# Conditioning vectors 6, 7 and 16 summed by TensorE in six halves instead of by VectorE in 24 blocks

## The reference

```python
cond = jax.nn.silu(c)
for l in range(DEPTH):
    m = (cond @ w_mod[l] + b_mod[l]).reshape(bsz, 3, 3, D_MODEL)
    x = x + 0.5 * m[:, 0, 2][:, None] * swiglu(adaln_in(x, norm_g[l, 0], m, 0), ...)
    h = adaln_in(x, norm_g[l, 1], m, 1) @ w_in[l]
    ...
    x = x + m[:, 1, 2][:, None] * (mix @ w_out[l])
    x = x + 0.5 * m[:, 2, 2][:, None] * swiglu(adaln_in(x, norm_g[l, 2], m, 2), ...)
```

## Time and profile before

| | us |
|---|---|
| median of 3 executions | 1642.44 (1641.61 to 1642.79) |
| the profiled execution, its own time | 1640.37 |
| its span in the trace | 1638.6 |
| TensorE matmuls busy | 1460.2 (89% of the span) |
| TensorE weight loads busy | 1375.4 (84%) |
| VectorE busy | 1361.1 (83%) |
| ScalarE busy | 982.0 (60%) |
| GpSimd busy | 81.9 (5%) |
| DMA | 420.31 MB, mean 257 GB/s over the span |

### The profile page before, as it was taken

The page is one execution under the profiler, slowest core; times in us unless marked ns, Lnnn a source line. Parts: engine busy times, 40 slices in busy tenths (PEclk is TensorE's granted clock), DMA queues, the critical chain, the costliest instruction groups (busy, mean ns, idle before and its releaser), DMA issues.

```text
span 1638.6 us, 27675 instructions
## 1 busy us (share of the span) xinstructions
PE 1460.2 (89%) x11160; PEld 1375.4 (84%) x11160; DVE 1361.1 (83%) x2231; ACT 982.0 (60%) x1640; POOL 81.9 (5%) x153
## 2 busy tenths in 40 slices
PE   7989758798979888887999999999999999988997
PEld 4888657697969786766998998987999899868997
DVE  2999758899999999877888988686988888687886
ACT  4555536555566446545676766547766766577665
POOL 0113010001101110000000000000000000000000
PEclk9999979899999999998999999899999999799999
DMA  9999563679968994427886877334777677435773
GB/s 387 366 385 415 204 235 140 251 289 333 392 237 323 402 395 155 154 77 284 284 317 227 281 276 262 123 148 170 267 273 272 231 276 278 162 116 199 274 273 129
DMA packets 84972, 420.31 MB, mean 257 GB/s; under 512 B 9363, under 2 KB 9795, under 8 KB 58094
## 3 DMA queue, kind: packets, MB, share of 16 engines
q1 hardware_dynamic: 64478, 343.48, 57.7%
q0 software_dynamic: 20368, 75.06, 12.1%
HBM read 417.38 MB, written 1.13 MB: 255 GB/s over the span
## 4 chain that ended last, share of the span: by engine, by line
PE 41%; DVE 6%; ACT 3%; DMA 2%; issue 1%; DVEq 0%
PE pw L626 13%; PE pw L627 13%; PE acc L626 6%; PE acc L627 6%; DVE low_p L1953 2%; DMA land_d<-stream 1%; ACT h_hi L1358 1%; PE acc L905 1%; PE pw L863 1%; ACT hi_p L1456 1%; ACT sq L1361 0%; PE acc L885 0%; DMA land_p<-stream 0%; ACT hi_d L1456 0%; DVE low_d L1953 0%
## 5 line engine op out<-in xcount | busy, mean ns | idle before, releaser
L626 PE MATMUL pw<-h_hi,hi_p 128*128 128x256 f32 x2976 | 754.3, 292 | 49.8 <-DVE low_p L1953 27.1
L627 PE MATMUL pw<-h_lo,low_p 128*128 128x256 f32 x2976 | 742.9, 288 | 0.0
L626 PEld LDWEIGHTS pw<-h_hi,hi_p 128*128 128x128 f32 x2976 | 587.1, 197 | 69.3 <-issue 30.1
L627 PEld LDWEIGHTS pw<-h_lo,low_p 128*128 128x128 f32 x2976 | 587.3, 197 | 0.4 <-issue 0.2
L1953 DVE SCALAR_TENSOR_TENSOR low_p<-hi_p,land_p 128x1024 fp32r<-128x1024 f32 x418 | 506.8, 1221 | 42.4 <-ACT hi_p L1456 42.1
L1456 ACT ACTIVATE hi_p<-land_p 128x1024 fp32r<-128x1024 f32 x418 | 434.0, 1047 | 64.4 <-DMA land_p<-stream 64.3
L626 PE MATMUL acc<-a_hi,hi_d 128*128 128x256 f32 x1376 | 343.2, 287 | 47.0 <-DVE low_d L1953 35.5
L627 PE MATMUL acc<-a_lo,low_d 128*128 128x256 f32 x1376 | 339.4, 284 | 0.0
L626 PEld LDWEIGHTS acc<-a_hi,hi_d 128*128 128x128 f32 x1376 | 265.4, 193 | 54.9 <-issue 41.1
L627 PEld LDWEIGHTS acc<-a_lo,low_d 128*128 128x128 f32 x1376 | 265.7, 193 | 0.0
L1953 DVE SCALAR_TENSOR_TENSOR low_d<-hi_d,land_d 128x1024 fp32r<-128x1024 f32 x205 | 249.4, 1218 | 11.7 <-ACT hi_d L1456 11.6
(11 more groups left out here) (354 smaller groups left out, 1665.7 us busy)
## 6 DMA issues: line engine op xcount, KB each, us to landing
land_p<-stream SPq DMA_DIRECT2D x207, 1024.0 KB, 5.1
land_d<-stream SPq DMA_DIRECT2D x209, 512.0 KB, 5.6
modw<-wmod POOLq DMA_DIRECT2D x116, 512.0 KB, 8.5
biasT<-wmod POOLq DMA_DIRECT2D x12, 512.0 KB, 4.2
biasT<-bias_rows POOLq DMA_DIRECT2D x3, 1536.0 KB, 11.4
modw<-wmod SPq DMA_DIRECT2D x8, 512.0 KB, 7.6
biasT<-wmod SPq DMA_DIRECT2D x8, 512.0 KB, 10.7
biasT<-bias_rows POOLq DMA_DIRECT2D x1, 3072.0 KB, 13.5
```

The source lines that it names most:

```text
L626: mm(o, lhs[0], rhs[0], start=start, stop=False, skip_group_check=True)
L627: return mm(o, lhs[1], rhs[1], start=False, stop=stop, skip_group_check=True)
```

## The change

Vectors 6, 7 and 16 leave VectorE's list (24 of its 128 blocks). Each is made by TensorE in two halves of 512 outputs: (6, 0), (6, 1), (7, 0), (7, 1), (16, 0), (16, 1). A half is four transfers of 512 KB, `half_sums` (eight calls, like those of `mod_first`), `half_copy` on ScalarE (128 x 512), `half_turn` on TensorE (four calls with one column) and `half_total` on VectorE (128 x 4). `STREAMED` puts (6, 0) and (6, 1) into steps 9 and 18 of stage 0 and (16, 0) and (16, 1) into steps 8 and 15 of stage 3: sums ahead of `up(j)`, copy behind `a_hi` of step j, turn behind `up(j + 1)`, total behind the gating product of step j + 1. (7, 0) takes the place of `keep_busy`; (7, 1) stands behind chunk 4. Their eight loads are issued ahead of the bias rows. The loads of the other four halves stand one by one between the loads for VectorE. In stage 0 VectorE now has 32 blocks, all eight of vector 6 being loaded there too; in stage 3 it has 32 instead of 40; in the mixer none.

The diff, cut:

```diff
-MOD_AT = {0: [[]] + spread(2, 7, 20, 4) + [[]], 2: [[]] * 3 + spread(8, 12, 17) + [[]] * 2,
-          3: [[]] * 3 + spread(12, 17, 17) + [[]] * 2, 5: [[]] * 3 + spread(17, 18, 18) + [[]]}
+MOD_AT = {0: [[]] + spread(2, 6, 20) + [[]], 2: [[]] * 3 + spread(8, 12, 17) + [[]] * 2,
+          3: [[]] * 3 + spread(12, 16, 17) + [[]] * 2, 5: [[]] * 3 + spread(17, 18, 18) + [[]]}
 RAW = (2, 3, 5)
-MOD_FIRST = {min(some[0] for some in MOD_AT[i] if some): i for i in (2, 5)}
-_ab = iter([(6, k) for k in range(4, KD)] + [(7, k) for k in range(KD)])
-MOD_AB = {(back, b): [next(_ab) for _ in range(count)] for back, b, count in AB_MODS}
+SUMMED = [2, 3, 4, 5] + list(range(8, 16)) + [17]
+HALVES = ((6, 0), (6, 1), (7, 0), (7, 1), (16, 0), (16, 1))
+HALF_NO = {half: x for x, half in enumerate(HALVES)}
+STREAMED = {0: {9: (6, 0), 18: (6, 1)}, 3: {8: (16, 0), 15: (16, 1)}}
+MOD_FIRST = {(8, 0): 2, (17, 0): 5}
...
+        def half_slot(x, n):
+
+            if HALVES[x] == (7, 0):
+                return modw[:, n, :]
+            if HALVES[x] == (7, 1) and n < 2:
+                return (proj[:, 18:22, :], qb[:])[n].rearrange("p c s -> p (c s)")
+            return wide_slot(n)
...
+            def load_half(g, h, n):
+
+                x = HALF_NO[g, h]
+                if (g, h) == (7, 0):
+                    pool.wait_ge(mod_used, 4 * KD - MODR + n + 1)
+                elif x:
+                    pool.wait_ge(mod_taken, 2 * KD + 4 * (x if (g, h) != (7, 1) else 2))
+                pool.dma_start(half_slot(x, n), wmod[g, 4 * h + n]).then_inc(half_load[x], 16)
...
-            load_mods(2 * KD, 5 * KD + 4)
+            load_mods(0, 6)
+            for n in range(4):
+                load_half(6, 0, n)
+                load_mods(6 + 2 * n, 8 + 2 * n)
+            load_mods(14, 20)
+            for n in range(4):
+                load_half(6, 1, n)
+                load_mods(20 + 2 * n, 22 + 2 * n)
...
-            load_mods(5 * KD + 4, 7 * KD)
+            load_mods(28, 4 * KD)
+            for n in range(4):
+                load_half(7, 0, n)
+            for n in range(4):
+                load_half(7, 1, n)
...
-                    load_mods(7 * KD, 17 * KD)
+                    load_mods(4 * KD, 8 * KD + 4)
+                    for n in range(4):
+                        load_half(16, 0, n)
+                        load_mods(8 * KD + 4 + 2 * n, 8 * KD + 6 + 2 * n)
+                    load_mods(9 * KD + 4, 10 * KD)
+                    for n in range(4):
+                        load_half(16, 1, n)
+                        load_mods(10 * KD + 2 * n, 10 * KD + 2 + 2 * n)
+                    load_mods(11 * KD, 12 * KD)
...
+                    if j in STREAMED.get(i, {}):
+                        half_sums(*STREAMED[i][j])
...
+                    if j - 1 in STREAMED.get(i, {}):
+                        half_turn(*STREAMED[i][j - 1])
...
+                    if n == 3:
+                        half_turn(7, 0)
+                    if n == 4:
+                        half_sums(7, 1)
+                half_turn(7, 1)
...
+            def half_sums(g, h):
+
+                x = HALF_NO[g, h]
+                bank = half_bank(x)
+                if x and x != 2:
+                    pe.wait_ge(half_read, x if x != 3 else 2)
+                pe.wait_ge(half_load[x], 64)
+                for n in range(4):
+                    for u in range(2):
+                        kc = n * 2 + u
+                        q = kc % 4 * 32
+                        m = mm(bank[q:q + 32, :], condz[:, kc, :], half_slot(x, n)[:, u * 512:(u + 1) * 512],
+                               start=(kc < 4), stop=(kc >= 4), skip_group_check=True)
+                    m.then_inc(mod_taken, 1)
+
+            def half_turn(g, h):
+
+                x = HALF_NO[g, h]
+                pe.wait_ge(half_copied, x + 1)
+                for c in range(4):
+                    m = mm(half_bank(x)[:, c:c + 1], half_row(x)[:, c * P:(c + 1) * P], ones[:, 0:1], start=(c == 0), stop=True, skip_group_check=True)
+                m.then_inc(half_turned, 1)
...
-                    keep_busy(pw[2], 7)
+                    half_sums(7, 0)
...
+                if j in STREAMED.get(i, {}):
+                    half_copy(*STREAMED[i][j])
...
+            def half_copy(g, h):
+
+                x = HALF_NO[g, h]
+                act.wait_ge(mod_taken, 2 * KD + 4 * x + 4)
+                fn(half_row(x), half_bank(x), ACT.Copy).then_inc(half_copied, 1)
...
+                        half_copy(7, 0)
+                    if n == 4:
+                        half_copy(7, 1)
...
+            def half_total(g, h):
+
+                o, x = PAR_AT["bmod"][0] + g * KD + 4 * h, HALF_NO[g, h]
+                dve.wait_ge(half_turned, x + 1)
+                v.tensor_tensor(modT[:, g, 4 * h:4 * h + 4], half_bank(x)[:, 0:4], par_s[:, o:o + 4], ALU.add).then_inc(half_read, 1)
...
+                    if j - 1 in STREAMED.get(i, {}):
+                        half_total(*STREAMED[i][j - 1])
...
-                mods_ab(3)
+                half_total(7, 1)
...
-                mods_ab(2)
+                half_total(7, 0)
...
-                mods_ab(8, 1)
```

More of the change, by code:

```diff
@@ L37 @@
 FIRST_MODS = 2
-AB_MODS = ((2, 2, 4), (3, 2, 4), (8, 1, 4))
 ONCE, TWICE = 63.0, 64.0
@@ L666, in filter_spectrum @@
                 spectrum(f_sum, f_dif).then_inc(filt_mm, 1)
-            def keep_busy(bank, count):
-                for _ in range(count):
-                    mm(bank[:, 0:P], ones[:], ones[:], start=True, stop=True)
             def spectrum(a, b):
@@ L2671 @@
     wmod = np.ascontiguousarray(a["w_mod"].reshape(2, D, 9, KD, P).transpose(0, 2, 3, 4, 1).reshape(NMOD, KD, P, D)[FIRST_SCALE])
-    for g in range(FIRST_MODS):
+    for g in list(range(FIRST_MODS)) + sorted({g for g, _ in HALVES}):
         rows = wmod[g].reshape(D, D).T.reshape(4, 2, P, 2, 512)
```

55 lines of the change are left out of this document (34 added, 21 removed).

## The result

The changed kernel takes 1655.93 us (median of four executions, 1653.74 to 1657.51) against 1642.03 (1641.30 to 1642.79) for the kernel before, timed beside it: ratio 1.0075, 95% interval 1.0057 to 1.0093. It is 13.9 us slower; 15 us faster was forecast. What happened is the rival that had 0.05: TensorE stands in line for its halves.

A forecast was written before the change was run, and what follows sets the result against it. VectorE was taken to bound the FFN stages, transfers close behind; in the first mixer three engines stood in line behind each other. -12 - 2 - 2.5 + 1.5 = -15.0 us gave a median of 1627.4 us (own range 1621 to 1634).

The forecast's parts named there:

- TensorE stands in line for its halves: Rival, chance 0.05: in stages 0 and 3 TensorE's queue waits for half loads; 8 us a half gives 1666 us.
- rival two: Rival, chance 0.18: transfers bound; stage 3 gives 0, stage 0 costs 5.3 us, the mixer gives 13: 1634.7 us.
- (14 - 1.5) / 4: Stages 0 and 3: stall per half, some 3 us, from which the rival of TensorE waiting for halves decides.
- Middle of the mixer, -12: First mixer up to its end part: earlier gather, triple and low splits save 12 us (9 to 15).
- (a) to (c): Mixer's middle: gather issued 8.8 us earlier, next triple sooner, low splits at about 222; chunk 9 starts 10.9 us earlier.
- (d): Mixer's middle: chunk 9's load, without block loads beside it, saves another 0 to 3.6 us, middle 1.6.
- (c): Mixer's middle: VectorE's low splits start at about 222, behind `half_total(7, 1)`, instead of 240.31; chunk 9 gains 10.9 us.
- End of the mixer, -2: Mixer's end: without the last four blocks, part of TensorE's 7.31 us idleness goes; 2 us saved, bounds 0 and 4.4.
- Stage 3, -2.5: Stage 3: VectorE gives 7.7 us, TensorE at most about 5, DMA 0 to 4; the smallest counts, 2.5 us saved.
- Stage 0, +1.5: Stage 0: 5.3 us for 2.1 MB more loads against 3.1 us of VectorE relief; 1.5 us lost.
- only arithmetic counts: Rival, chance 0.14: DMA keeps up, VectorE's whole relief arrives; 3.1 + 7.7 + 16 = 26.8 us saved: 1615.6 us.
- transfers are the bound: Rival, chance 0.18: stage 3 gives 0, stage 0 costs 5.3 us, the mixer gives 13: 1634.7 us.

The follow-up runs named there:

- the cut end: Kernel before the change, with its last four conditioning blocks of the mixer, (7, 4) to (7, 7), cut to 8 of 1024 columns, load and sum: 1638.01 us.
- early loads: Changed kernel with the loads of the four FFN-stage halves issued earlier, those of (16, 0) in stage 2, sums at the same steps: 1625.91 us.
- combined: Changed kernel with vector 6's halves summed at steps 12 and 20 of stage 0, and vector 16's loads issued earlier: 1623.35 us, repeated 1624.31.
- later halves: Changed kernel with halves summed at steps 12 and 20 of stage 0, 11 and 18 of stage 3, load order kept: 1627.44 us.

## Why the prediction was wrong

**The step that failed** is in the rival "TensorE stands in line for its halves": "The last load of a half is issued about three steps ahead, 18 us, and a conditioning load's median is 8.5 us", hence "a slack of some 9 us" and a chance of 0.05. Both numbers were wrong in the same direction. The lead was 8.6, 9.2, -0.4 and 2.6 us, because I counted steps on one list. This is the wait that the sum had put at nothing. `half_sums` stands at step 8 of TensorE, but the loads are released by VectorE's blocks, and TensorE comes to `up(j)` up to two steps before VectorE comes to step j: when TensorE stood at step 8 (523.08) VectorE was ending step 6 (its `a_hi` at 518.87, that of step 7 at 525.28), and it is a block of that step behind which the fourth load stands in GpSimd's list. And a median was taken for a wait that ends with the last of four loads: 11.8 to 16.6. The median itself was not far off for single loads in a full stretch (8.4 for the 36 issued from 500 to 625 us before, 9.8 for the 30 into `modw` from 60 to 180); what it left out is that each load of a half goes out beside others and lands later than the one before it. Together a lead of 5.0 on average against 14.9 us to landing, which is the 9.9 of wait. The arithmetic behind it was fair: 8 us a half was to give 1666; 9.9 gave 1656, since it counted rival two's cost and no recovery, and some 0.7 for each us came out. Its threshold, "(14 - 1.5) / 4", doesn't use that rival's costs as it says: with 5.3 for stage 0 it is 2.2 us a half.

**Middle of the mixer, -12 (9 to 15):** right in mechanism, a little small. Up to the load issued at 299.04 (298.45 before) it gained 15.4. (a) to (c), 10.9 less 0.7 for the added work, measured 12.4; (d), "0 to 3.6 us, middle 1.6", was the small one: the next load went out 16.9 us earlier, 4.5 more, and the cut end shows that these 4.5 us are the conditioning loads beside it. In (c) `half_total(7, 1)` came when it was forecast, "at about 222": 41 us behind the last `a_hi`, measured 39.6. VectorE stood waiting 6.41 us for it, which cost nothing, since the next triple landed only at 239.28, 42.4 behind.

**End of the mixer, -2 (0 to 4.4):** measured 4.0; TensorE's idle 7.31 became 2.75, the upper bound. How much of it comes from the blocks is open: cutting them alone left 4.84 us of idle time and gave 0.8 there, so the forecast's reason for the 2 us isn't borne out.

**Stage 3, -2.5:** the reasoning of three limits was right and its smallest term too generous. Without any wait the stage takes 136.6 to 137.2, so nothing is gained. VectorE's relief was there (7.7 forecast; the stage is 9.3 shorter when the loads are left out), TensorE's 8.2 counted nothing visible, so "leaves at most about 5" was wrong, and the transfers took everything: "at most 4 gained, and 0 if 400 is all" was 0. With the loads of (16, 0) in stage 2 the stage gains 1.7 in early loads and 4.5 to 5.5 in the five kernels built on combined.

**Stage 0, +1.5 (-3.1 to +5.3):** 4.4 to 5.1 without waits, inside the bounds and near the upper, but not for the reason given. The kernel without vector 6 has VectorE's four blocks less, 2.1 MB less to load and no copies; it gains 3.0, where the blocks alone were put at 4.6 (3.1 with the copies). The loads, "2.1 MB more, or 5.3 us", cost no more than the scatter (143.3 against 142.2); TensorE's 8.2, taken as covered by 10.5 of waits, is what costs, some 7.

With the waits gone the kernel takes 1626.8 to 1627.4, the forecast 1627.4; but that is a coincidence of a mixer 5.4 us better and FFN stages some 6 worse. Against "only arithmetic counts" speak the last two points; "transfers are the bound" was right for stage 3, not for stage 0.

Two smaller points. The figure of 358 GB/s is said to hold when both cores of a pair stream; this kernel runs on one core, so the traced 400 doesn't speak against it, as the prediction has it. And the narrow matmul groups between full-width ones, which the sum left unpriced, show no gap where nothing is waited for: in later halves one starts at 106.19 and takes 1.92 us, and the next full-width row starts at 108.05.
